# mLSTM mixer of a two-block decoder step: from features on partitions to tokens on partitions

## The reference, cut to what matters

```python
proj = x @ w_in
qk, v, o, gates, z = jnp.split(proj, [o1, o2, o3, o4], axis=-1)
qk = jax.nn.silu(_causal_depthwise_conv(qk, conv_w, conv_b))
...
    s_qk = jnp.einsum('bhtd,bhsd->bhts', qx, kx) * jnp.exp(dmat - m_t[..., None])
    num = (w_inter[..., None] * jnp.einsum('bhtd,bhdv->bhtv', qx, c_st)
           + jnp.einsum('bhts,bhsv->bhtv', s_qk, vx))
    den = w_inter * jnp.einsum('bhtd,bhd->bht', qx, n_st) + jnp.sum(s_qk, axis=-1)
    h_out = num / jnp.maximum(jnp.abs(den), jnp.exp(-m_t))[..., None]
...
cell = _rmsnorm(cell.astype(x.dtype), head_norm.reshape(ML_HEADS, ML_V)).reshape(b, s, ML_WIDTH)
hcell = jax.nn.sigmoid(o) * cell
return (hcell * jax.nn.silu(z)) @ w_out
```

## Time and profile before

| | |
|---|---|
| median of 3 runs | 1955.01 us (1954.74 to 1955.89) |
| the profiled execution | 1956.35 us, its span in the trace 1954.9 us |
| instructions | 26280 |
| DMA | 353.28 MB, mean 181 GB/s |

### The profile page before, as it was taken

One profiled execution on the slowest core, in us unless ns is written; L12 is line 12 of the kernel. 1 busy time (PEld: TensorE's weight loads), 2 busy tenths in 40 slices (PEclk: granted clock), 3 DMA queues, 4 the chain that ended last, 5 costly groups with the idle time before them and its releaser, 6 DMA issues.

```text
span 1954.9 us, 26280 instructions
## 1 busy us (share of the span) xinstructions
PE 1947.3 (100%) x10316; PEld 1667.4 (85%) x10316; DVE 1370.0 (70%) x2046; ACT 1021.2 (52%) x1497; POOL 0.2 (0%) x4
## 2 busy tenths in 40 slices
PE   9999999999999999999999999999999999999999
PEld 7889988988888888898888888888888888888887
DVE  6756777987557676899687877588666544666654
ACT  5645555675456754575565655444444334444443
POOL 0000000000000000000000000000000000000000
PEclk9999999999999999999999999999999999999999
DMA  8554325555543555546544345555555555555563
GB/s 325 176 191 173 130 99 185 181 203 180 194 151 130 182 187 192 183 166 218 193 150 145 108 168 180 197 189 193 191 187 185 212 195 192 194 194 183 187 232 108
DMA packets 51711, 353.28 MB, mean 181 GB/s; under 512 B 5652, under 2 KB 7196, under 8 KB 9860
## 3 DMA queue, kind: packets, MB, share of 16 engines
q1 hardware_dynamic: 50016, 348.84, 49.7%
q10 hardware_dynamic: 1572, 2.75, 0.4%
HBM read 349.47 MB, written 2.11 MB: 180 GB/s over the span
## 4 chain that ended last, share of the span: by engine, by line
PE 92%; DVE 5%; ACT 1%; issue 1%; DMA 0%; SPq 0%; ACTq 0%; DVEq 0%
PE bank L1168 92%; DVE WL L2107 2%; ACT WH L1600 0%; DVE AR L2284 0%; DVE ft L2882 0%; DMA mu_acc<-in_sgu 0%; DVE AR L2397 0%; DVE XP L2280 0%; DVE AR L2394 0%; DVE XP L2382 0%; PE bank L1313 0%; DVE AR L2273 0%; DVE AR L2308 0%; DVE AR L2307 0%; ACT XP L1731 0%
## 5 line engine op out<-in xcount | busy, mean ns | idle before, releaser
L2107 DVE TENSOR_TENSOR WL<-raw,WH 128x1024 fp32r<-128x1024 f32 x649 | 785.1, 1222 | 339.7 <-ACT WH L1600 336.7
L1600 ACT ACTIVATE WH<-raw 128x1024 fp32r<-128x1024 f32 x649 | 682.9, 1057 | 609.8 <-PE bank L1168 603.8
L1168 PE MATMUL bank<-XP,WH 128*128 128x512 f32 (+2 forms) x2096 | 668.2, 393 | 0.4 <-DVE XP L2382 0.2
L1168 PEld LDWEIGHTS bank<-XP,WL 128*128 128x128 f32 x2016 | 378.1, 188 | 81.1 <-issue 0.7
L1168 PE MATMUL bank<-WH,FP 128*128 128x512 f32 x1408 | 434.7, 389 | 0.1
L1168 PE MATMUL bank<-XP,WL 128*128 128x256 f32 (+1 forms) x2016 | 409.4, 278 | 0.1
L1168 PEld LDWEIGHTS bank<-XP,WH 128*128 128x128 f32 (+1 forms) x2096 | 328.8, 188 | 8.0 <-issue 1.4
L1168 PEld LDWEIGHTS bank<-WH,FP 128*128 128x128 f32 x1408 | 264.3, 188 | 56.1 <-DVE WL L2107 1.0
L1168 PE MATMUL bank<-WL,FP 128*128 128x512 f32 x704 | 273.9, 389 | 0.0
L1168 PE MATMUL bank<-WH,AP 128*128 128x512 f32 x704 | 217.2, 389 | 0.0
L1168 PEld LDWEIGHTS bank<-WH,AP 128*128 128x128 f32 x704 | 132.1, 188 | 27.5
(11 more groups left out here) (330 smaller groups left out, 1722.3 us busy)
## 6 DMA issues: line engine op xcount, KB each, us to landing
raw<-in_W SPq DMA_DIRECT2D x326, 1024.0 KB, 4.7
out<-XT ACTq DMA_DIRECT2D x8, 256.0 KB, 2.0
raw<-in_W SPq DMA_DIRECT2D x3, 512.0 KB, 7.0
X<-in_x SPq DMA_DIRECT2D x3, 512.0 KB, 12.6
AR<-rv SPq DMA_DIRECT2D x1, 1024.0 KB, 6.3
cst<-in_cst SPq DMA_DIRECT2D x1, 899.5 KB, 11.5
raw<-in_W SPq DMA_DIRECT2D x2, 256.0 KB, 4.5
AR<-in_sgu SPq DMA_DIRECT2D x1, 512.0 KB, 6.1
```

The lines of the kernel that those rows point to most:

```text
L1168: return pe.matmul(o, lhsT, rhs, start=start, stop=stop)
L1600: ac.activation(w_slot(WH, s), raw_half(hf), ACT.Copy).then_inc(s_hi, 1)
L2107: tt(w_slot(WL, s), raw_half(pl.half_of[s]), w_slot(WH, s).bitcast(F32), ALU.subtract).then_inc(s_lo, 1)
```

## The change

Everything between the values and the output projection is held with tokens on partitions.

- `o` and `mz` become token-major: 4 blocks of 16 tiles of 512 columns each, in two banks per block.
- `m0` spreads one row only (256 columns). The bound of the denominator now comes per token through two more tiny transposes in `gate turn`.
- `m4`: `At` is stationary and V moves, 256 features and a column of ones behind them (`by_head`, 257 columns), three matmuls: tokens 0 to 127 into bank 5, tokens 128 to 255 into bank 6 with two. The denominator is column 257. Both banks serve every head.
- `m5` is two plain copies on DVE and two squares on ACT that sum along the row (`accum_out`). `m6`, `m7`, `m5 sum` and the two ones matmuls are gone; denominators and norms of all heads are made at once from 16 columns (`cell sums`).
- The gated product is made in place in `O` (`mz cell`, `mz out`). TensorE then turns it, four transposes of 128x128 for each head (`mz turn`), ACT and DVE read the bank, multiply by `head_norm` and write high and low part of `HP` (`mz low`). Three quarters of the turns are in the section `mz`, the last two heads in the first steps of `wo1`.

```diff
-    t_blocks("ml_w_in", [r(4096 + 128 * b, 128) for b in range(16)], DM)
-    t_blocks("ml_w_in", [r(6160 + 128 * b, 128) for b in range(16)], DM)
+    t_blocks("ml_w_in", [r(4096 + 512 * n, 512) for n in range(4)], DM)
+    t_blocks("ml_w_in", [r(6160 + 512 * n, 512) for n in range(4)], DM)
...
-           Stage("vm", 4, 16, "act", 0, 512), Stage("o", 16, 16, "dve"), Stage("mz", 16, 16, "dve"),
+           Stage("vm", 4, 16, "act", 0, 512), Stage("o", 4, 16, "dve", 0, 512), Stage("mz", 4, 16, "act", 0, 512),
...
-    p.big = [0, 1]
-    op, zp = p.proj(st["o"]), p.proj(st["mz"])
-    fill = then(op, itertools.islice(zp, 4))
-    p.pipe(8, [None, "m1", "m3", "m4", "m5", "m6", "m7"], fill, 68, (1, 3, 4, 5),
-           (4, (1, "m0"), 3, 2, (5, "m5 sum"), 6, 1, (4, "m5 squares"), 5),
-           [3] * 11 + [4] * 3)
+    p.big, p.turn = [0, 1, 2, 4], 0
+    def o_after(b):
+        return {1: [("o", b, 0)], 4: [("o", b, 1)]}
+
+    def mz_after(b):
+        steps = {2: [("mz", b, 0)], 5: [("mz", b, 1)], 8: [("mz turn", 2 * b)], 9: [("mz low", 2 * b)],
+                 11: [("mz turn", 2 * b + 1)], 12: [("mz low", 2 * b + 1)], 14: [("mz cell", 2 * b + 2)],
+                 15: [("mz cell", 2 * b + 3)]}
+        return steps if b else {0: [("mz cell", 0)], 1: [("mz cell", 1)], **steps}
+
+    fill = then(by_token("o", {}), by_token("mz", {**o_after(3), 13: [("cell sums", 0)], 15: [("o end", 0)]}))
+    p.pipe(8, [None, "m1", "m3", "m4", "m5"], fill, 76, (1, 3, 4), (4, 2, (1, "m0"), 1, 3))
...
-                    mm(bank[3][:, 0:512], E3[0:72, 128 * h:128 * (h + 1)], G3[0:72, :], True, True).then_inc(s_m0, 1)
+                    mm(bank[3][:, 0:T], E3[0:72, 128 * h:128 * (h + 1)], G3[0:72, :], True, True).then_inc(s_m0, 1)
...
-                    for c in range(2):
-                        vo = h * 256 + c * 128
-                        mm(N[:, c * T:(c + 1) * T], Vm[:, vo:vo + 128], a[:, 0:256], True, False)
-                        mm(N[:, c * T + 128:(c + 1) * T], Vm[:, 2048 + vo:2048 + vo + 128], a[:, 256:384], False, True)
-                    mm(bank[7][:, 0:T], ones, a[:, 0:256], True, False)
-                    mm(bank[7][:, 128:T], ones, a[:, 256:384], False, True).then_inc(s_m5, 1)
+                    v = [by_head(Vm, half, h) for half in range(2)]
+                    mm(bank[5][:, 0:VW], a[:, 0:128], v[0], True, True)
+                    mm(bank[6][:, 0:VW], a[:, 128:256], v[0], True, False)
+                    mm(bank[6][:, 0:VW], a[:, 256:384], v[1], False, True).then_inc(s_m5, 1)
+                    free[5] = free[6] = s_mnum, h + 1
+                elif what == "mz turn":
+                    b = TURN_BANK[h]
+                    take(b)
+                    pe.wait_ge(s_zg, 2 * (h // 2) + 2)
                     for c in range(2):
+                        for half in range(2):
+                            ins = pe.transpose(bank[b][:, c * T + 128 * half:c * T + 128 * half + 128],
+                                               o_head(half, h)[:, 128 * c:128 * c + 128], ident)
...
-                elif what == "m6":
-                    b = cell_bank[h]
-                    take(b)
-                    pe.wait_ge(s_m7, h + 1)
-                    mm(bank[b][:, 0:T], ones, sqh[h % 2][:, 0:T], True, True).then_inc(s_m8, 1)
...
+                elif what == "o out":
+                    b, half = divmod(n, 2)
+                    e = eo[n % 2]
+                    ac.wait_ge(*done("o", b))
+                    if n >= 2:
+                        ac.wait_ge(*outed("o", b - 1, half))
+                    chain(ac.activation(e, bank[pl.bank_of["o", b, half]][:, :], ACT.Abs))
+                    chain(ac.activation(e, e, ACT.Exp, scale=-1.0))
+                    ac.activation(e, e, ACT.Ln, bias=ones[:, 0:1]).then_inc(s_oln, 1)
+                    if n >= 1:
+                        o_exp(n - 1)
...
+                elif what == "o out":
+                    b, half = divmod(n, 2)
+                    dv.wait_ge(s_oln, n + 1)
+                    stt(o_of(half, b), bank[pl.bank_of["o", b, half]][:, :], 0.0, eo[n % 2], ALU.min,
+                        ALU.subtract).then_inc(s_out["dve"], 1)
```

More of the change, by code:

```diff
@@ L593, in plan @@
     wo = p.proj(st["wo1"])
-    for n in (16, 17):
+    steps = {0: [("mz", 3, 0)], 1: [("mz", 3, 1)], 4: [("mz turn", 6)], 5: [("mz low", 6)],
+             6: [("mz turn", 7)], 7: [("mz low", 7)]}
+    for at in range(8):
+        for what in steps.get(at, ()):
+            if what[0] == "mz":
+                p.out(st["mz"], what[1], what[2])
+            else:
+                say(*what)
         go(wo, 1)
-        say("mz end", n)
     go(wo)
@@ L1400, in pe_program @@
-            for what, n in pl.steps["mz"]:
-                if what == "tile":
-                    tile(n)
-            for what, n in pl.steps["wo1"]:
-                if what == "tile":
-                    tile(n)
-                elif what == "wo1 out" and n == 5:
+                    v = [by_head(Vm, half, h) for half in range(2)]
+                    mm(bank[5][:, 0:VW], a[:, 0:128], v[0], True, True)
+                    mm(bank[6][:, 0:VW], a[:, 128:256], v[0], True, False)
+                    mm(bank[6][:, 0:VW], a[:, 256:384], v[1], False, True).then_inc(s_m5, 1)
@@ L1866, in act_program @@
-            for what, n in pl.steps["mz"] + pl.steps["wo1"]:
-                if what == "hi":
-                    hi(n)
+                    ac.activation(D[:, 256:384], D[:, 256:384], ACT.Exp, bias=aT[:, 8 + h:9 + h]).then_inc(s_m4, 1)
+                elif what == "m5":
+                    ac.wait_ge(s_mnum, h + 1)
+                    for half in range(2):
+                        if h:
+                            ac.wait_ge(s_msq, 2 * h - 1 + half)
+                        ac.activation(sqh[half], by_head(HN, half, h)[:, 0:T], ACT.Square,
+                                      accum_out=ssq[:, 8 * half + h:8 * half + h + 1]).then_inc(s_msq, 1)
+                elif what == "o out":
+                    b, half = divmod(n, 2)
[8 more added lines that the diff above has]
+                        o_exp(n - 1)
+                elif what == "cell sums":
+                    ac.wait_ge(s_mden, 1)
+                    ac.activation(den, den, ACT.Square, scale=(256 * EPS) ** 0.5).then_inc(s_mden, 1)
+                    ac.wait_ge(s_mden, 3)
+                    rstd(rsh, ssq, 256, 4).then_inc(s_mrs, 1)
@@ L2459, in dve_program @@
                     stt(ab, fp, -1.0, fp, ALU.mult, ALU.min).then_inc(s_gates, 1)
+                    for half in range(2):
+                        o = VW * 8 * half
+                        dv.memset(Vm[:, o:o + 8 * VW].rearrange("p (h v) -> p h v", h=8)[:, :, T:VW], 1.0)
                     chain(dv.memset(G3[0:72, :], 0.0))
@@ L2468, in dve_program @@
                     chain(dv.tensor_tensor_scan(Mx, ai, ai, 0.0, ALU.max, ALU.max))
-                    chain(ts(GR[:, 0:T], Mx, -1.0, None, ALU.mult))
-                    chain(tt(GR[:, T:2 * T], GR[:, 0:T], Fc, ALU.subtract))
+                    chain(ts(GR, Mx, -1.0, None, ALU.mult))
+                    tt(GM, GR, Fc, ALU.subtract)
                     for o in (0, 32):
@@ L2477, in dve_program @@
                     dv.wait_ge(s_gates, 4)
-                    dv.tensor_copy(aT, bank[5][:, 0:16]).then_inc(s_gates, 1)
-            def o_log(n):
-                o = blk(O, n)
-                dv.wait_ge(s_oln, n + 1)
-                stt(o, o, 0.0, eo[n % 2], ALU.min, ALU.subtract).then_inc(s_olg, 1)
-            for what, n in pl.steps["mlstm"]:
+                    dv.tensor_copy(small[:, 0:32], bank[5][:, 0:32]).then_inc(s_gates, 1)
+            for what, n in pl.steps["mlstm"] + pl.steps["mz"] + pl.steps["wo1"]:
                 h = n
@@ L2531, in dve_program @@
[L2531 to L2553 removed]
+                    for half in range(2):
+                        ins = dv.tensor_copy(by_head(HN, half, h), bank[5 + half][:, 0:VW])
```

237 lines of the change are left out of this document (103 added, 134 removed).

## The result

The changed kernel takes 1943.89 us (median of 4 runs, 1943.76 to 1944.38); the kernel before, on the same chip, 1955.25 us (1954.74 to 1955.89). The ratio is 0.9942, with a 95% interval of 0.9925 to 0.9959: faster, by 11.4 us. The forecast was 1946.4 with a range of 1944.0 to 1950.0.

What follows compares the result with a forecast made beforehand. The prediction took PE as the bound, busy for 1947.3 of 1954.9 us. Its PE terms sum to -9.1 us, plus 0.5 for waits: -8.6 from 1955.0, giving 1946.4 us, with a range of 1944.0 to 1950.0.

Steps and rivals of the forecast that it cites:

- tiles: In `o` and `mz`, 128 token-major tiles of six matmuls replace 512 tiles: 174.6 us for 177.9, minus 3.3 us.
- m0: In the eight heads, half the columns: 0.12 us for 0.23, minus 0.9 us in all.
- m4: In the eight heads, 771 fp32 columns instead of 1152: 1.31 us for 1.96, minus 5.2 us in all.
- m6: In the eight heads, this matmul is gone: 8 x 0.42 us, minus 3.4 us.
- turns: In `mz turn`, 32 added transposes of 128x128 on PE at 0.11 us each: plus 3.5 us.
- gates' turns: Two extra little transposes of the gates on PE: at most plus 0.2 us.
- waits: PE waiting for late weights, mainly at `o` block ends and the start of `wo1`: plus 0.5 us, bounds nothing and 4.
- rival A: Weights come late at the four `o` block ends and the start of `wo1`: 2 to 6 us, 1948.4 to 1952; chance 0.13.
- B: In `m4`, odd rows of V stream at half the rate: 10.5 us on top of the forecast, 1956.9; chance 0.05.
- C: Each transpose in `mz turn` costs its full printed 0.27 us: 5.1 us more, 1951.5; chance 0.03.
- D: Slower: at `o` block ends the whole ACT and DVE queue is pushed back, 12.6 us of waits, above 1959; chance 0.03.
- E: Work leaves PE but the time stays, because something other than PE sets the pace in the stretch; chance 0.02.

Runs made afterwards that it cites:

- e5: Kernel before with only the `o` and `mz` matmuls changed: every four tiles become six matmuls of 512 columns; 1951.76 us (ratio 0.9983).
- e7: Kernel after with the two ones matmuls put back into `m4`; 1950.24 us.
- e6: Kernel before without the `m6` matmuls, the root taken of unsummed squares; 1951.18 us (ratio 0.9980).
- e8: Kernel after with every turn's transposes issued twice; 1948.39 us.
- e1: Kernel before run again unchanged, for a second profile; 1955.25 us (ratio 1.0002).
- e2: Kernel after run again unchanged, for a second profile; 1944.39 us (ratio 0.9946 to the kernel before).
- e13: Kernel before with the six-matmul form of `o` and `mz` and without the `m6` matmuls; 1947.72 us (ratio 0.9964).
- e12: Kernel after with two more ACT copy passes of 512 columns in each `o out`; 1946.68 us (ratio 0.9958 to the kernel before).
- e9: Kernel before with three warm-up matmuls of 512 columns replaced by one of 512 and 22 of 16 columns; 1961.74 us (ratio 1.0035).
- e11: Kernel after with three warm-up matmuls of 512 columns replaced by one of 512 and 17 of 16 columns; 1951.00 us (ratio 0.9980 to the kernel before).
- e14: Kernel before with six-matmul `o` and `mz`, no `m6`, and the ones matmuls of `m4` cut to one of a single column; 1945.64 us (ratio 0.9954).

## Why the prediction was right, and where it was not

| term | forecast | measured | from |
|---|---|---|---|
| tiles | -3.3 | -3.4; -3.7 without its new waits | e5 |
| `m0` | -0.9 | -0.9 | 0.12 us in the timeline |
| `m4` | -5.2 | -5.0 to -5.2 | e7; 1.31 us in the timeline |
| `m6` | -3.4 | -2.8; -3.6 without its new waits | e6 |
| turns | +3.5 | +3.3 | e8 |
| gates' turns | +0.2 | +0.1 | the `vm` window |
| waits | +0.5, the gap kept | -0.7 | distances at `m4` in before; none over in after |
| sum, local | -8.6 | -10.5 to -10.7; measured whole -10.1 | |
| late stretch | nothing | -1.5 to -2.0 | e1 and e2; the first profiles |

**What bounds the kernel.** Right: it is PE's own time, term after term, and e5 and e6 add (e13, to 0.1 us). Reading prices from distances between starts, not from the printed times, gave `m0`, `m4` and the turns to 0.01 us. It holds for `m6` as well: e6's 2.8 us are only 0.35 a head, but with the 0.8 us of new waits at `m4` they are 3.6, or 0.45 against the 0.42 that were read. The forecast's sum on PE alone, -9.1, with -0.7 for the waits in place of +0.5, gives -9.8, 0.3 from the -10.1 measured.

**The step that failed, first part: the waits.** The forecast said that what ACT and DVE lose "is worth nothing by itself, since PE waits for neither now", and kept the gap of 0.44 us, "that nothing the profile knows explains". The gap was a wait for DVE and cost 0.7 us. Part of that hid in the 6.4 us that the forecast gave to `m1` as what was left over: by distances `m1` takes 0.66 us (1.12 less 0.46), 5.3 for eight. It would have grown to 1.9 us as the form and `m6` gave PE's time back (e13), and with the new place of the normalizer and the lighter `m5` there is none. So the term is -0.7 where +0.5 was put: 1.2 of the 1.5 us that the local stretch missed. What the forecast feared instead, the ends of the `o` blocks, cost nothing. The chain was worked out as 5.2 us against 5.45, some 0.2 us of room. At the first end 1.0 us was left, since an `m1` on PE stood between the two blocks and ACT got its start meanwhile; at the last end, with the squares of head 6 ahead on ACT as the forecast had it, 0.24. e12 shows that 1.3 us more on the chain bring rival A. Its chance of 0.13 was fair.

**The second part: the late stretch.** The sum had no term behind the stretch of the change. There PE's instruction fetch (one packet of 16 KB on queue q8) and the `in_sgu` load, which lies on PE's path, meet or miss each other. In all 14 profiles that keep the order of the steps, the late stretch is 166.4 to 167.3 us where the fetch falls from 0.4 us before to 5.1 us after the load's first issue (six of them), and 165.2 to 165.4 where it falls elsewhere (eight). The landing of the load's second part is 6.5 to 7.3 us in the first case and 5.8 to 6.0 in the second. That the packet is PE's is read from the way it moves with PE's instructions: 80 more of them ahead brought it 7 to 8 us earlier (e9). e9 shows the effect without any change in the work behind the warm-up, and e11 shows it in the other direction; e13 had the rule on record before it ran, and so had e14; in both the fetch fell outside and the stretch was short. A theory that an earlier issue makes the load faster falls with e9, whose issue is the latest of all (1050.93) and whose stretch is short. Instructions removed or added anywhere ahead move the fetch, so this gain came with the change but is not a merit of its form: e7 and e8 lost it again. What delays the load when a fetch is near was not shown. In before, e1 and e5 the issue on SP is itself long (1.4, 1.3 and 1.3 us), in e7, e8 and e11 only the landing is. A contest for the DMA engines fits both, but it is argued from times alone. The edge between +5.1 (e11, inside) and +5.5 (e6, outside) rests on those two.

**The rivals.** B is excluded: the three matmuls of 257 columns, at odd starts for every other head, take 1.31 us. C is excluded by e8. D and E did not come. A is near, by e12. What the forecast's own range of 1944.2 to 1948.5 lacked is the late term: with -8.6 - 1.5 for the two stretches it would have been 1944.9, and with the waits at -0.7 as well, 1943.7. Either of the two steps alone would have left the time in the range; the late gain was luck, since where the fetch falls was in no term.

**Open.** The measured terms, each cleared of waits, add to 0.4 to 0.6 us more than the local stretch gained; where it went is not known. e14 is accounted for: the cut of the ones matmuls was worth 2.1 us there. An undisturbed `m4`, by the distance from `WH` to `WL`, fell from 2.42 to 2.00 us, 3.4 for eight heads, and the waits grew by 1.2 over e13. The expectation had this matmul of a single column at 0.06 us a head; by the distances it is 0.23 (0.65 for the two ones matmuls, of which only 0.42 went). So the time above both theories is waits and this price, and K and L were both wrong for it.

## What to carry to other kernels

When the bound engine has a short wait that the profile puts down to nothing, look at which step on another engine ends 0.1 us before it goes on, and at which bank or buffer that step frees: such a wait grows with every cut of the bound engine's work, and goes with the buffer's owner. Measure such a wait by distances too: its idle time of 0.44 us was 0.68 of PE's. Read as distances between starts, the forecast's terms came within 0.3 us of ten here once the wait was put right, so a total that is off by more has a cause somewhere else; compare starts of the same instructions before and behind the change, to the end of the program. A one-off load on the critical path far from the change can gain or lose 1.0 to 2.1 us when the instruction stream moves, and a comparison of two kernels to within 0.1% should name it.

## What was not expected of the hardware

- One instruction fetch of PE near a load on the critical path goes with 1.0 to 2.1 us more in that stretch (table above).
- At the start of the program PE runs at about half its later rate while the row of its granted clock reads 1.00: in e9 the pairs of tile matmuls take 0.64 us up to 17.2 us and 0.35 behind it. With small matmuls ahead this lasts longer: in before the pairs take 0.35 from 7.2 us on.
- A small fp32 matmul is not paid by its columns. In e9 the 44 records of 16 columns stand 0.21 us apart, 0.43 for a matmul in two records, where 1.70 ns a column would give 0.03; their weight loads stand 0.21 us apart as well (43 in 9.30 us). In the middle of e14 the matmul of a single column takes 0.23 us by the distances above. That its two loads set this, at half the rate in e9, fits both and was not tried.
- Moving operands of 257 fp32 columns stream at the same 1.70 ns a column as those of 256, and the four heads whose V starts at an odd word take no longer than the other four: from `WH` to `WL` each of the eight `m4` takes 1.76 to 1.77 us.
